# Value projection of a transformer block ahead of the norm's root: the root applied per token at the copy out

## The reference, cut to what matters

```python
h = rms_norm_2(x, norm_pre[l])   # x * rsqrt(mean(x*x) + EPS) * norm_pre, per token
u = h @ w_in[l]
(a_q, a_k, a_v, a_z, b_q, ...) = jnp.split(u, split_points, axis=-1)
...                              # three attentions, gates, w_out, post norm
x = x + jax.nn.sigmoid(x @ w_ple_gate[l]) * (p[l] @ w_ple_proj[l])
```

## Time and profile before

| | us |
|---|---|
| median of 3 runs | 2617.38 (2616.23 to 2618.15) |
| the profiled execution, its own time | 2616.12 |
| its span in the trace | 2614.3 |
| TensorE busy | 2502.5 (96% of the span), 12134 matmuls |
| VectorE busy | 1432.4 (55%) |
| ScalarE busy | 1113.9 (43%) |
| GpSimd busy | 41.8 (2%) |
| the chain that ended last | 90% TensorE, 6% VectorE, 2% ScalarE |

### The profile page before, as it was taken

How to read it: one execution, slowest core, us unless ns; L and a number is a source line. 1 busy time by engine, 2 the same in 40 slices (tenths; PEclk the granted TensorE clock), 3 DMA queues, 4 the chain that set the end, 5 groups by cost and what they waited for, 6 DMA issues and landing times.

```text
span 2614.3 us, 32447 instructions
## 1 busy us (share of the span) xinstructions
PE 2502.5 (96%) x12134; PEld 1984.8 (76%) x12134; DVE 1432.4 (55%) x2221; ACT 1113.9 (43%) x1975; POOL 41.8 (2%) x28
## 2 busy tenths in 40 slices
PE   5998999999999899999999999999999999999998
PEld 2886788888776678888877777778877777777886
DVE  6778665556656653433346744554454664455445
ACT  4575434433535534433434534442343554344243
POOL 2000000000000000000000000000010000000001
PEclk8999999999999999999999999999999999999999
DMA  6435366666221113222222122222322121222233
GB/s 231 153 106 194 135 209 202 209 201 216 73 89 61 46 65 106 97 97 97 97 97 73 57 74 68 73 77 89 105 81 90 65 71 65 69 73 77 97 98 104
DMA packets 77901, 280.35 MB, mean 107 GB/s; under 512 B 8640, under 2 KB 8896, under 8 KB 77504
## 3 DMA queue, kind: packets, MB, share of 16 engines
q1 hardware_dynamic: 60624, 218.02, 24.7%
q10 hardware_dynamic: 17136, 60.37, 7.0%
HBM read 276.26 MB, written 2.10 MB: 106 GB/s over the span
## 4 chain that ended last, share of the span: by engine, by line
PE 90%; DVE 6%; ACT 2%; issue 1%; DMA 0%; ACTq 0%; SPq 0%; DVEq 0%
PE ps L220 25%; PE ps L222 24%; PE ps L221 24%; PE ps L1690 2%; PE ps L1777 2%; PE ps L1750 1%; PE ps L1593 1%; PE ps L1694 1%; PE ps L1115 1%; DVE wl L215 1%; PE ps L1650 1%; PE ps L486 1%; PE ps L487 1%; PE ps L1899 1%; PE ps L491 1%
## 5 line engine op out<-in xcount | busy, mean ns | idle before, releaser
L215 DVE TENSOR_TENSOR wl<-raw,wh 128x1024 fp32r<-128x1024 f32 x374 | 459.2, 1228 | 730.1 <-ACT wh L212 730.1
L220 PE MATMUL ps<-xh,wl 128*128 128x512 f32 x1744 | 698.4, 400 | 16.2 <-DVE wl L215 12.3
L212 ACT ACTIVATE wh<-raw 128x1024 fp32r<-128x1024 f32 x374 | 394.9, 1056 | 680.0 <-PE ps L222 633.2
L222 PE MATMUL ps<-xh,wh 128*128 128x512 f32 x1744 | 682.2, 391 | 0.0
L221 PE MATMUL ps<-xl,wh 128*128 128x512 f32 x1744 | 681.8, 391 | 0.0
L220 PE MATMUL ps<-bh,wl 128*128 128x512 f32 x1158 | 458.3, 396 | 13.3 <-DVE wl L215 7.1
L222 PE MATMUL ps<-bh,wh 128*128 128x512 f32 x1158 | 451.9, 390 | 0.0
L221 PE MATMUL ps<-bl,wh 128*128 128x512 f32 x1158 | 451.8, 390 | 0.0
L220 PEld LDWEIGHTS ps<-xh,wl 128*128 128x128 f32 x1744 | 328.7, 188 | 134.4 <-issue 45.8
L222 PEld LDWEIGHTS ps<-xh,wh 128*128 128x128 f32 x1744 | 328.8, 189 | 70.3
L221 PEld LDWEIGHTS ps<-xl,wh 128*128 128x128 f32 x1744 | 329.1, 189 | 65.9 <-issue 1.4
(11 more groups left out here) (306 smaller groups left out, 2540.3 us busy)
## 6 DMA issues: line engine op xcount, KB each, us to landing
raw<-in_w SPq DMA_DIRECT2D x388, 512.0 KB, 3.2
bA<-in_ada ACTq DMA_DIRECT2D x74, 512.0 KB, 4.6
bC<-in_ada SPq DMA_DIRECT2D x9, 512.0 KB, 11.1
bD<-in_ada ACTq DMA_DIRECT2D x8, 512.0 KB, 4.8
bS<-in_ada ACTq DMA_DIRECT2D x8, 512.0 KB, 5.0
bS<-in_attn_bias ACTq DMA_DIRECT2D x8, 512.0 KB, 3.3
bC<-in_ada ACTq DMA_DIRECT2D x6, 512.0 KB, 4.1
bD<-in_ada SPq DMA_DIRECT2D x5, 512.0 KB, 14.9
```

Of the source, the lines that this page charges most:

```text
L212: e.activation(wh[p][:], raw[p][:], ACT.Copy).then_inc(s_hi, 1)
L215: e.tensor_tensor(wl[p][:], raw[p][:], wh[p][:].bitcast(F32), ALU.subtract)\
L220: e.matmul(out, wl[p][:, blk, 0:M], xhi, start=start, stop=False)
L222: return e.matmul(out, wh[p][:, blk, 0:M], xhi, start=False, stop=stop)
```

## The change

A layer's values are now computed from h x norm weight, without the root, and the root is applied as the scale of the four copies. It has these parts:

- `ahead` and `ahead_low` (new): hi = h x gain on ScalarE, low = h x gain - hi on VectorE. They run in the eight units before a head: into `xh`, `xl` at layer 0, into `bh`, `bl` at layer 1, which are free there.
- The head: value tile 0 (12 matmuls), the first sums, the last sums, value tile 1, the spread of the root, value tiles 2 to 7. The splits of weights stand between: the first behind the last value tile in the program (on ScalarE and VectorE ahead of the normed tiles), the second behind normed tile 3, the third behind 5, the fourth behind 7.
- The normed tiles are written to `xh`, `xl` during this. At layer 0, where value tiles read the same buffer, ScalarE's copy for tile k waits for value tile k.
- Lambda, the bias transfer and the value copies follow. The query unit waits for normed tiles one by one.

The diff, cut to its core:

```diff
+            def ahead(s, m, gain, hi, lo):
+                if act:
+                    done(e.activation(hi[:, m, :], hk(m), ACT.Copy, scale=gain(m)), f"{s}ahi{m}")
+            def ahead_low(s, m, gain, hi, lo):
+                if dve:
+                    need(f"{s}ahi{m}")
+                    done(e.scalar_tensor_tensor(lo[:, m, :], hk(m), gain(m), hi[:, m, :].bitcast(F32), ALU.mult, ALU.subtract),
+                         f"{s}alo{m}")
...
                             square(nxt, m, hk(m), bTk(m), lambda: e.wait_ge(s_bank[bk], used + 2))
+                            if early:
+                                ahead(nxt, m, *early)
                             if m >= 2:
                                 add_square(nxt, m - 1, bTk)
+                            if early and m:
+                                ahead_low(nxt, m - 1, *early)
+                            if early and m == KD - 1:
+                                ahead_low(nxt, m, *early)
                         if not up and (dve or (act and end)):
                             split(u0 + 2, 0, i)
...
-            mlp("M1", 88, None, "L0n", rotary_table)
+            mlp("M1", 88, None, "L0n", rotary_table, (lambda k: v("pre_g", k), xh, xl))
...
+                            if it.ready:
+                                need(f"{it.ready}hi{kt}")
+                                need(f"{it.ready}lo{kt}")
                             mm = mm3(ps[bank][:], p, kt, xh[:, kt, :], xl[:, kt, :], kt == 0, kt == KD - 1)
...
-                rstd_of(n + "n", KD, D, rows_of)
-                normed(n + "n", hk, KD, lambda k: v("pre_g", 8 * l + k), None, xh, xl, rows_of, n + "nrstd")
+                ah, al = (bh, bl) if l else (xh, xl)
+                def value_tile(kt):
+                    if pe:
+                        p, k = place(U[0] + kt // 2, 0, 0)
+                        if kt % 2 == 0:
+                            e.wait_ge(s_lo, 2 * k + p + 1)
+                        need(f"{n}nahi{kt}")
+                        need(f"{n}nalo{kt}")
+                        ...
+                        for t in range(NT):
+                            r = slice(P * t, P * t + P)
+                            if kt == 0:
+                                e.wait_ge(s_bank[2 + t], BK[2 + t] + 1)
+                            e.matmul(ps[2 + t][:], ah[:, kt, r], wlk, start=kt == 0, stop=False)
+                            e.matmul(ps[2 + t][:], al[:, kt, r], whk, start=False, stop=False)
+                            mm = e.matmul(ps[2 + t][:], ah[:, kt, r], whk, start=False, stop=kt == KD - 1)
+                        if kt % 2:
+                            mm.then_inc(s_unit, 1)
+                        else:
+                            done(mm, f"{n}vu{kt}")
+                def value_split(a):
+                    if act:
+                        unit_read(U[0], 0, a)
+                    split(U[0] + 2, 0, a)
+                value_tile(0)
+                rstd_of(n + "n", KD, D, rows_of, (lambda: None, lambda: value_tile(1)))
+                for kt in range(2, KD):
+                    value_tile(kt)
+                value_split(0)
+                if dve:
+                    need(n + "nrstd")
+                for k in range(KD):
+                    if act and l == 0:
+                        if k % 2:
+                            unit_read(U[0], 0, k // 2)
+                        else:
+                            need(f"{n}vu{k}")
+                    normed_tile(n + "n", k, hk, lambda k: v("pre_g", 8 * l + k), None, xh, rows_of)
+                    if k:
+                        put_lo(n + "n", k - 1, rows_of, None, xh, xl)
+                    if k == 3:
+                        value_split(1)
+                    if k == 5:
+                        value_split(2)
+                put_lo(n + "n", KD - 1, rows_of, None, xh, xl)
+                value_split(3)
...
-                for a in range(4):
-                    ...
-                        for kk in range(2):
-                            kt = 2 * a + kk
-                            need(f"{n}nhi{kt}")
-                            need(f"{n}nlo{kt}")
-                    ...
-                    split(U[0] + 2, 0, 0)
-                    U[0] += 1
                 for t in range(NT):
                     if act:
-                        done(e.activation(bT[:, t, :], ps[2 + t][:], ACT.Copy), f"{n}v{t}")
+                        done(e.activation(bT[:, t, :], ps[2 + t][:], ACT.Copy, scale=sm[:, t:t + 1]), f"{n}v{t}")
...
-                heads = [[Unit("copy", f"{n}aq{t}", dq(t), scored(t)), ...
+                heads = [[Unit("copy", f"{n}aq{t}", dq(t), scored(t), ready=n + "n" if t == 0 else None), ...
...
                     if l == 0:
+                        early = (lambda k: v("pre_g", 8 + k), bh, bl)
                         square("L1n", m, hk(m), bDk(m), lambda: need(f"{s}h{m}"))
+                        ahead("L1n", m, *early)
                         if m >= 2:
                             add_square("L1n", m - 1, bDk)
+                        if m:
+                            ahead_low("L1n", m - 1, *early)
+                        if m == KD - 1:
+                            ahead_low("L1n", m, *early)
```

More of the change, by code:

```diff
@@ L907, in h_ready, with mlp @@
                         e.wait_ge(s_bank[b], BK[b] + 1)
-            def mlp(s, g2, ada0, nxt, between):
+            def mlp(s, g2, ada0, nxt, between, early=None):
                 u0, b = U[0], list(BK)
@@ L1857, in program @@
                 rows_of = bDk if l else bTk
-                rstd_of(n + "n", KD, D, rows_of)
-                normed(n + "n", hk, KD, lambda k: v("pre_g", 8 * l + k), None, xh, xl, rows_of, n + "nrstd")
+                ah, al = (bh, bl) if l else (xh, xl)
+                NB[0] += 1
+                def value_tile(kt):
[5 more added lines that the diff above has]
+                        need(f"{n}nalo{kt}")
+                        whk, wlk = (x[p][:, 4 * (kt % 2):4 * (kt % 2) + 4, :].rearrange("p a b -> p (a b)") for x in (wh, wl))
+                        for t in range(NT):
[9 more added lines that the diff above has]
+                            done(mm, f"{n}vu{kt}")
@@ L1860, in program @@
+                put_lo(n + "n", KD - 1, rows_of, None, xh, xl)
+                value_split(3)
+                U[0] += 4
                 if dve:
@@ L1883, in program @@
                     e.dma_start(bT[:, 4:8, :], io["da_bias"]).then_inc(s_bias, 16)
-                NB[0] += 1
-                for a in range(4):
-                    if pe:
-                        p, k = place(U[0], 0, 0)
-                        e.wait_ge(s_lo, 2 * k + p + 1)
-                        for kk in range(2):
-                            kt = 2 * a + kk
-                            need(f"{n}nhi{kt}")
-                            need(f"{n}nlo{kt}")
[L1893 to L1904, removed]
-                    split(U[0] + 2, 0, 0)
-                    U[0] += 1
                 for t in range(NT):
                     if act:
-                        done(e.activation(bT[:, t, :], ps[2 + t][:], ACT.Copy), f"{n}v{t}")
+                        done(e.activation(bT[:, t, :], ps[2 + t][:], ACT.Copy, scale=sm[:, t:t + 1]), f"{n}v{t}")
                 dq, dk = (lambda t: bC[:, t % 2, :]), (lambda t: bC[:, 2 + t % 2, :])
@@ L1921, in scored @@
                     return (lambda: need(f"{s}{4 * t - 5}sc1")) if t > 1 else None
-                heads = [[Unit("copy", f"{n}aq{t}", dq(t), scored(t)), Unit("copy", f"{n}ak{t}", dk(t), scored(t))] for t in range(4)]
+                heads = [[Unit("copy", f"{n}aq{t}", dq(t), scored(t), ready=n + "n" if t == 0 else None), Unit("copy", f"{n}ak{t}", dk(t), scored(t))] for t in range(4)]
                 silu = [Unit("silu", f"{n}az{t}", bS[:, t, :]) for t in range(4)]
```

## The result

The changed kernel takes 2598.93 us (2596.95 to 2600.85, 4 runs), the kernel before 2616.81 beside it (2614.95 to 2618.15, 4 runs). The ratio is 0.9931, 95% interval 0.9919 to 0.9944: 17.9 us faster, where 17.3 were forecast. The forecast of 2600.1 is 1.2 over the median, and the range held it.

The account below looks back on a forecast made before the run. TensorE was taken to bound, with waits and slow clock at two heads. Savings of 8.0 and 9.3, together 17.3 us, with early work costing nothing, took the 2617.38 median to 2600.1; range 2597.5 to 2604.9.

Parts of the forecast that it names:

- What bounds: TensorE's matmul row bounds; it stands or runs slowly at the heads of the second block's two layers.
- The stretch: From the end of dense work to line 220 at each head: 33.05 and 34.34 us become 25.05.
- The waits at the seams: Value tile 0's start: bank 3 idles some 0.3 us at head one; weight split 0.3 late at head two.
- The clock: TensorE's clock stays full over both heads, as in the post-norm; a fall costs 1.44 to 1.70 us a head.
- rival one: Clock falls at both heads, giving 2603.2 us, or at one head, 2601.7; chance 0.13.
- The cost of the early copies: 16 ScalarE copies of 0.63 us and 16 VectorE subtractions of 0.75 before the heads, covered, cost nothing.
- The weakest step: In head two's gate units ScalarE idles 1.04 us before its tanh, so a 0.63 copy fits.
- Moved splits: Value weight splits stand between normed tiles; tightest is the fourth unit's, ready 2.5 us before TensorE asks.
- rival two: A split or normed tile comes late ahead of the third value pair or in the query unit; 2604.9 us, chance 0.10.
- Rival three: Early work in the 16 units before the heads has no cover, costs 22.9 us, giving 2623.0; chance 0.03.
- Rival four: At the heads, value tile 0 cannot start before the sums, being late by 3 us; 2605 us, chance 0.02.

Follow-up runs that it names:

- seam kernel: Changed kernel, value tile 0 fills bank 3 last and the last but one gate unit splits weights before its early copy; 2602.10 us, again 2601.57 us.
- Experiment 4: Changed kernel with value tile 1 moved from behind the sums to behind the spread, tile 0 staying ahead of the sums; 2604.61 us, ratio 0.9955.
- Experiment 7: Changed kernel with each early copy and each early subtraction done twice, the second behind the first; 2606.14 us, ratio 0.9960.
- experiment 8: Changed kernel with ScalarE copying normed tile 3 seven times more ahead of its second value split; 2605.18 us, ratio 0.9957.
- experiment 6: Kernel before, with unread matmuls in the gaps of both heads and the first value split ahead of lambda's steps; 2613.04 us, ratio 0.9987.

## Why the prediction was right, point by point

- **What bounds** was right: 17.4 of 17.9 us lie in the two stretches. The rest of the trace behind head one moved by a few tenths, and the 1.1 ahead of it is not of the change.
- **The time** was forecast as 2600.1 and measured as 2598.93. Of the 1.2 us between them 0.6 is the kernel before, 2616.81 in the comparison where 2617.38 was assumed; the gain, 17.3 and 17.9, is off by the other 0.6. The lower end of the range is stated as 2597.5; its own terms (0.6, 0.5 and 1.2 under 2600.1) give 2597.8. The result lies inside either.
- **The stretch**, 25.05 forecast at both, 24.99 and 25.01 measured. That it came so close is in part luck, for the terms were off in both directions: the sums in one piece take 1.70 (1323.36 to 1325.06), not 1.62, and the spread 0.81 (1327.91 to 1328.72), not 0.89; what is left for refills is 0.40, not 0.48. The waits at the seams were forecast at 0.3 each. They measure 0.32 and 0.34: from start to start 0.55 (1320.62 to 1321.17) and 0.57, less the pace.
- **The clock** stayed at 1.00, as chosen against rival one, but the reason was too weak, so this was in part luck. The post-norm's row stood for sums of 0.8 us apart; here they are 1.7 us in one piece. In the seam kernel sums of the same form were followed by a fall, for 1.7 us at head two (26.39 against the 24.7 that were expected warm): the price of rival one. A page of the Trainium skill ("TensorE: Matmul & The Clock Gate", "A second HAM failure mode: psum-queue depth-cycling") says that short idle spells between groups of matmuls can bring the clock down. The changed kernel's traces do not bear that out (1.00 in the three windows shown, with idle spells of 0.16 and 0.19 us ahead of them). Experiment 4 agrees with it at head one (0.86 us of idling, then 2.07 for the spread) and not at head two (1.50 us, then 1.16). In the seam kernel the clock fell behind sums with no idle time ahead of them.
- **The cost of the early copies** was mis-sized: 0.708 us, where I had bounded it by 0.60 and 0.68 and took 0.63. The subtraction was 0.746 (0.75 taken). The value copies with a scale take 0.690, by their median, 0.097 more than the 0.593 of before, not at most 0.08. The Trainium skill ("ScalarE: Activation LUTs", "What ACT_TABLE_LOAD costs") puts a scale that is read from memory, one value per partition, at about 93 ns on top of one that stands in the instruction; the 97 ns between the two copies agree. The instructions of the changed kernel, by line: count, ns min/median/max:

```profile
L533 ACT ACTIVATE xh<-h,vec x8: 707/708/709, 1283.9 to 1321.7; 128x512 fp32r<-128x512 f32 x8
L539 DVE SCALAR_TENSOR_TENSOR xl<-h,vec,xh x8: 742/746/752, 1288.4 to 1322.5; 128x512 fp32r<-128x512 f32 x8
L1958 ACT ACTIVATE bT<-ps,sm x8: 680/690/698, 1349.3 to 1986.2; 128x512 f32<-128x512 f32 x8
```

- **The weakest step** is the cover ahead of head two: "ScalarE idles 1.04 before its tanh; 0.63 fits". That idle time was of the last but one gate unit, when ScalarE had caught up. In the units before it was behind TensorE, and what counts there is the round through ScalarE and VectorE against TensorE's: 4.20 became 4.81, of 5.44. It still fits, so the sum was not hurt, but the spare is 0.63 us a unit, needed to catch up, and not a lead of two splits. Experiment 7 used it up with a price of 5.0 us at that head.
- **Moved splits.** Spare time 2.5 forecast for the fourth unit; 2.2 and 2.4 in the trace, and experiment 8 paid what went beyond. So rival two named the right place; it did not come about by itself.
- **Rival three** (no cover, 22.9 us) is wrong at head one, where twice the work costs nothing. At head two a cost of that kind begins somewhere between the present amount and twice as much. Rival four did not occur: value tile 0 starts within 0.35 us.

What makes up the 17.4, by experiments: about 4.9 for not waiting for normed tiles; about 4.6 for the clock (measured in the kernel before, where the normed wait still stands, and at head two with a short fall left in it). The rest, 7.9, no run measures by itself. It fits the idle times ahead of sums and root that value work now fills: 1.44 and 0.87 in the earlier trace rows, 2.74 in the earlier trace rows and the 0.86 of this row of the kernel before, together 5.9. What is then left may be the fall that experiment 6 still had at head two, which is not shown.

```profile
1971.11 2.08 PE L433 MATMUL ps<-cst,sm 128*128 128x128 f32 x8 [0.86 <-DVE sm L429]
```

The parts are not strictly additive, since what is slow depends on what waits.

## What to carry to other kernels

A factor that is per row of a product's output can be applied when the output is copied out. The gain then is not the wait for the normed input alone (4.9 of 17.4 us here) but that work is free to stand between the steps of the root, which also keeps TensorE's clock up. Before work is put onto an engine that "has idle time", follow the chain of work that comes round once a unit, through every engine it passes, and compare its length with the bounding engine's time for a unit, above all in a stage where it starts late. The engine's idle time alone does not show the spare. A gap closed at one engine exposes the next late thing, here a weight split, so move that with it.

## What the runs showed of the hardware

In the two kernels that have two traces, the falls of the granted clock at the heads, or their absence, came again in the second trace. The program and its clock had the same distance from each other there (345.7 to 345.8 us from the clock's last rise to the end of the dense work ahead of head one, in all four), so this does not show what another starting point would bring. The seam kernel, whose sums start 0.3 us sooner behind the dense work, had a fall at head two in both traces (0.76 over 7 us against 1.00, 1.4 us longer); the changed kernel had none. A fall need not follow the longest idle time: 0.86 us of idling brought one, 1.50 us did not, and the seam kernel's had no idle time before it. So a change that saves a few tenths in one place can lose one or two microseconds elsewhere, as the seam kernel did: its heads were 0.9 us longer together, for the clock, and 0.5 more went between them; its time was 1.9 longer (2601.57 against 2599.72).
